# Normed rows of x by a product with a diagonal, later pad clearing, and projections of units 1 to 5 as three rounded products

## The reference, cut to what is computed

```python
h = rms_norm(x, norm1_w)
u = h @ w_in
rnn_x, rnn_gate, q, k, v, iq, ik, iw, g = jnp.split(u, offsets, axis=-1)
q = rms_norm(q.reshape(B, T, N_HEADS, HEAD_DIM), q_norm_w)     # 16 heads of 64
k = rms_norm(k.reshape(B, T, N_KV_HEADS, HEAD_DIM), k_norm_w)  # 4 heads of 64
ik = rms_norm(ik, idx_k_norm_w)
# index scores: relu(iq . ik) weighted by iw; the 64 best keys of each query are kept
# attention over them: softmax(q . k * scale) @ v
```

## Time and profile before

| | us |
|---|---|
| median of 3 runs (1203.43 to 1207.15) | 1205.72 |
| the profiled execution | 1205.84 |
| its span, first to last instruction | 1204.0 |
| TensorE busy | 1111.9 (92%) |
| VectorE busy | 501.4 (42%) |
| ScalarE busy | 396.3 (33%) |
| mean DMA rate over the span | 257 GB/s |

### The profile page before, as it was taken

How to read it: one execution, slowest core, us unless ns; L and a number is a source line. 1 busy time by engine, 2 the same in 40 slices (tenths; PEclk the granted TensorE clock), 3 DMA queues, 4 the chain that set the end, 5 groups by cost and what they waited for, 6 DMA issues and landing times.

```text
span 1204.0 us, 16125 instructions
## 1 busy us (share of the span) xinstructions
PE 1111.9 (92%) x6491; PEld 785.2 (65%) x6491; DVE 501.4 (42%) x965; ACT 396.3 (33%) x761; POOL 16.3 (1%) x28
## 2 busy tenths in 40 slices
PE   6999999999999999999999996998978897879786
PEld 5778898888999999798678885432323232323231
DVE  3657776586766655576975523000100010101011
ACT  2432665934666444565345402000100000001000
POOL 3000000000000000000000000000000000000000
PEclk9999999999999999999999998899999999999999
DMA  7444543244456676345223786699999999999996
GB/s 228 155 145 151 188 141 140 89 140 140 170 180 193 157 184 165 139 157 180 84 73 138 275 354 250 256 428 428 428 427 427 428 427 427 428 429 427 427 423 251
DMA packets 94066, 309.42 MB, mean 257 GB/s; under 512 B 6000, under 2 KB 39032, under 8 KB 82040
## 3 DMA queue, kind: packets, MB, share of 16 engines
q1 hardware_dynamic: 93256, 307.42, 66.2%
q0 software_dynamic: 496, 1.07, 0.4%
q10 hardware_dynamic: 256, 0.10, 0.0%
HBM read 307.53 MB, written 1.05 MB: 256 GB/s over the span
## 4 chain that ended last, share of the span: by engine, by line
PE 72%; DMA 22%; DVE 3%; ACT 1%; issue 1%; SPq 0%; ACTq 0%; DVEq 0%
PE bank L435 71%; DMA parts_room<-in_w_up 7%; DMA arena<-in_w_down 4%; DMA arena<-in_w_up 3%; DMA parts_room<-in_w_down 3%; DMA ring<-in_w_down 3%; DMA xh<-in_w_down 2%; PE bank L644 0%; DMA arena<-in_x 0%; DVE arena L1567 0%; DVE parts L1632 0%; DVE roots_room L1604 0%; PE bank L548 0%; DVE hidden_parts L1840 0%; DVE arena L2157 0%
## 5 line engine op out<-in xcount | busy, mean ns | idle before, releaser
L1228 ACT ACTIVATE parts<-ring 128x512 fp32r<-128x512 f32 x288 | 179.0, 629 | 196.5 <-PE bank L435 195.4
L1632 DVE TENSOR_TENSOR parts<-ring,parts 128x512 fp32r<-128x512 f32 x288 | 193.2, 690 | 117.2 <-ACT parts L1228 115.8
L435 PE MATMUL bank<-parts 128*128 128x256 f32 (+1 forms) x1872 | 239.8, 288 | 0.8 <-issue 0.6
L435 PEld LDWEIGHTS bank<-parts 128*128 128x128 f32 x1872 | 230.1, 191 | 13.2 <-issue 10.1
L435 PE MATMUL bank<-hidden_parts,parts 128*128 128x256 f32 x1024 | 164.9, 283 | 0.0
L435 PE MATMUL bank<-arena 128*32 128x512 f32 (+5 forms) x516 | 148.6, 499 | 9.2 <-DMA ring<-in_w_down 2.7
L435 PE MATMUL bank<-arena,roots_room 128*32 128x512 f32 x400 | 131.4, 601 | 12.1 <-DMA ring<-in_w_gate 3.7
L435 PEld LDWEIGHTS bank<-hidden_parts,parts 128*128 128x128 f32 x1024 | 141.4, 192 | 0.1
L2144 DVE TENSOR_TENSOR sqr<-bank,arena 128x512 f32<-128x512 f32 x8 | 5.2, 686 | 269.9 <-ACT arena L1531 269.9
L435 PEld LDWEIGHTS bank<-arena 128*128 128x128 f32 (+3 forms) x516 | 74.6, 192 | 54.6 <-issue 43.3
L435 PE MATMUL bank<-ring,roots_room 128*32 128x512 f32 x224 | 95.6, 593 | 7.8 <-DMA xh<-in_w_up 4.0
(11 more groups left out here) (298 smaller groups left out, 1068.0 us busy)
## 6 DMA issues: line engine op xcount, KB each, us to landing
ring<-in_w_in SPq DMA_DIRECT2D x22, 2048.0 KB, 8.0
arena<-in_w_gate SPq DMA_DIRECT2D x14, 2048.0 KB, 34.9
arena<-in_w_down SPq DMA_DIRECT2D x13, 2048.0 KB, 37.3
arena<-in_w_up SPq DMA_DIRECT2D x11, 2048.0 KB, 37.0
ring<-in_w_ff_in SPq DMA_DIRECT2D x8, 2048.0 KB, 7.9
ring<-in_w_ff_out SPq DMA_DIRECT2D x8, 2048.0 KB, 9.0
parts_room<-in_w_up SPq DMA_DIRECT2D x8, 2048.0 KB, 36.8
ring<-in_w_gate SPq DMA_DIRECT2D x7, 2048.0 KB, 34.6
```

The source lines that it names most:

```text
L435: return nc.tensor.matmul(o, lhsT=l, rhs=r, start=first, stop=last)
L1228: A(w_part[0][:, p % PIECES], piece_of(n, p), ACT.Copy).then_inc(S("pieces rounded"), 1)
L1632: X.tensor_tensor(w_part[1][:, p % PIECES], piece_of(n, p), w_part[0][:, p % PIECES].bitcast(F32), ALU.subtract).then_inc(S("pieces split" ...
```

## The change

1. Start: `xdiag` (two 128x128 diagonals with 1/rms of the tokens) takes the place of `xnormed`. The 16 transposes of normed rows become 16 float32 products `xtok` by `xdiag`. Two of the four groups of x transposes are made ahead of them, two behind. The first half of unit 0 is loaded by a DMA of its own, and half (0,0) waits for its four banks of `hT` one by one.
2. GpSimd clears `ikpad` and `kpad` only when the first vectors have been turned.
3. Units 1 to 5 become `dense_split`, so ACT and DVE round and split ten more halves, and `hT` is split at once.
4. Queries are no longer normed on DVE: ACT writes them to `qT` times the norm weight, `q1_stats` puts the mean squares of all heads with tokens on partitions (128x32), and 1/rms goes as `q1_scale` into the scale of the softmax.
5. `kpad` is filled by `pad_keys(g)`, two copies at a time, behind later halves; `select_keys` is cut into `select_rounds` and `key_bias` between the halves' rests. Index scores use bank 7 once only.

The core of the diff:

```diff
-            for b in range(4):
+            def turn_x(b):
                 ps = take(4 + b, ("x", b))
...
+            turn_x(0)
+            turn_x(1)
             for b in range(4):
                 ps = take(b, ("h", b))
...
-                        last = nc.tensor.transpose(ps[:, c:c + P], xnormed[:, t, k * P:k * P + P], ident)
+                        last = mm(ps[:, c:c + P], xtok[:, t, k * P:k * P + P], xdiag[:, t, :])
                 last.then_inc(S("h turned"), 1)
+            turn_x(2)
+            turn_x(3)
...
+            pe.wait_ge(S("first half loaded"), 16)
...
+                    if t == 0 and k % 2 == 0:
+                        wait_taken(("h", k // 2))
...
-            dense(1, 0, hT)
+            dense_split(1, 0, 0)
...
+            def q1_stats(i):
...
+                for j in range(2):
+                    for t in range(TT):
+                        c, at_c = j * T + t * P, 8 * i + 4 * t + 2 * j
+                        last = mm(ps[:, at_c:at_c + 2], sqr[:, i % 2, c:c + P], mean_64[:, 0:P:64])
...
-            dense(5, 1, hT)
+            dense_split(5, 1, 0)
...
-            A(xnormed[:, 0, :], xtok[:, 0, :], ACT.Copy, scale=xscale[:, 0:1]).then_inc(S("x 0 scaled"), 1)
+            A(xdiag[:, 0, :], ident, ACT.Copy, scale=xscale[:, 0:1]).then_inc(S("x 0 scaled"), 1)
...
             half(4, 0)
-            root_of(("heads", 5), 512, "head stats", 6)
+            act.wait_ge(S("head stats"), 6)
+            empty(A(q1_root, ps("q1 stats")[:, 0:32], ACT.Sqrt, bias=eps), "q1 stats")
+            round_half(8)
+            pad_keys(1)
             half(4, 1)
+            round_half(9)
+            pad_keys(2)
             half(5, 0)
-            round_half(0)
+            round_half(EARLY)
+            pad_keys(3)
             half(5, 1)
...
-            X.tensor_scalar(xnormed[:, 1, :], xtok[:, 1, :], xscale[:, 1:2], None, ALU.mult).then_inc(S("x 1 scaled"), 1)
+            X.tensor_scalar(xdiag[:, 1, :], ident, xscale[:, 1:2], None, ALU.mult).then_inc(S("x 1 scaled"), 1)
...
+            rest_of_half(6)
+            select_rounds(0, range(0, 8))
+            key_bias(0)
+            rest_of_half(7)
+            wait_taken("q1 stats")
+            link(X.reciprocal(q1_scale, q1_root))
+            link(X.tensor_scalar(q1_scale, q1_scale, SC1, None, ALU.mult))
+            select_rounds(1, range(0, 2))
+            rest_of_half(8)
+            select_rounds(1, range(2, 5))
+            rest_of_half(9)
+            select_rounds(1, range(5, 8))
+            key_bias(1)
+            rest_of_half(EARLY)
...
-            G.memset(kpad, 0.0)
-            G.memset(ikpad, 0.0)
-
-            pool.wait_ge(S("h turned"), 4)
+            pool.wait_ge(S("vectors 0 turned"), 1)
+            G.memset(ikpad, 0.0)
+            G.memset(kpad, 0.0)
```

More of the change, by code:

```diff
@@ L402, in done @@
             return S(dense_at[job][0]), dense_at[job][1]
-        split_halves = [(n, h) for n in range(6, 12) for h in range(2)]
+        split_halves = [(n, h) for n in range(1, 12) for h in range(2)]
+        EARLY = 10
         LATE = len(split_halves)
@@ L607, in index_scores @@
                 wait_taken((1, t // 2))
-                ps = take(4 + a % 4, ("index", a))
+                ps = take(4 + a if a < 4 else 4 + a % 3, ("index", a))
                 mm(ps[:, 0:2 * keys], iqT[:, t, q * P:q * P + P], ikpad[:, :, 0:keys]).then_inc(S("index scores"), 1)
-            dense(2, 0, hT)
+            dense_split(2, 0, 0)
             for a in range(4):
                 index_scores(a)
-            dense(2, 1, hT)
-            head_stats(2)
-            for a in range(4, 8):
+            dense_split(2, 1, 0)
+            for a in range(4, 7):
                 index_scores(a)
[L618 to L625, removed]
-            dense(5, 1, hT)
+            q1_stats(0)
+            dense_split(3, 0, 0)
+            index_scores(7)
+            q1_stats(1)
+            filter_layer(2)
+            dense_split(3, 1, 0)
+            q1_stats(2)
+            dense_split(4, 0, 0)
+            q1_stats(3)
+            dense_split(4, 1, 0)
+            dense_split(5, 0, 0)
+            dense_split(5, 1, 0)
             def att_scores(a):
@@ L1261, in _, with pad_keys @@
                 A(h_part[0][:, k, :], hT[:, k, :], ACT.Copy).then_inc(S("h rounded"), 1)
-            act.wait_ge(S("pads set"), 1)
-            wait_taken((0, 0))
-            for g in range(KV_HEADS):
+            round_half(0)
+            half(0, 0)
+            act.wait_ge(S("lambda ready"), 1)
+            A(lw[1], lw[1], ACT.Exp).then_inc(S("lambda exp"), 1)
+            hidden_sine(0)
+            half(0, 1)
+            act.wait_ge(S("ik"), 1)
+            A(sqr[0:64, 1, 0:T], ps("ik")[0:64, 0:T], ACT.Square).then_inc(S("head squares"), 1)
+            root_of(("heads", 0), 512, "head stats", 1)
+            round_half(1)
+            half(1, 0)
+            root_of(("heads", 1), T, "head stats", 2, 64)
+            round_half(2)
+            half(1, 1)
+            round_half(3)
+            hidden_sine(1)
+            def pad_keys(g):
                 for side in range(2):
@@ L1302, in _ @@
                 for j in range(4):
[L1303 removed]
+                    c = 8 * g + 4 * q + 2 * (j % 2) + j // 2
+                    A(prob[:, j, 0:keys], prob[:, j, 0:keys], ACT.Exp, bias=nmx[:, j:j + 1], scale=q1_scale[:, c:c + 1],
                       accum_out=rsum[:, j:j + 1]).then_inc(S("exps"), 1)
@@ L1576, in _, with rest_of_h @@
                 empty(X.tensor_copy(xT[:, 2 * b:2 * b + 2, :], pair(bank[4 + b][:, :])), ("x", b))
+            def rest_of_h(src, h_set, k):
+                dve.wait_ge(S("h rounded"), KD * h_set + k + 1)
+                X.tensor_tensor(h_part[1][:, k, :], src[:, k, :], h_part[0][:, k, :].bitcast(F32), ALU.subtract)\
+                    .then_inc(S("h split"), 1)
+            for k in range(KD):
+                wait_taken(("h", k // 2))
+                rest_of_h(hT, 0, k)
             dve.wait_ge(S("vectors 0 turned"), 1)
```

117 lines of the change are left out of this document (59 added, 58 removed).

## The result

The changed kernel takes **1194.31 us** (median of 4 runs, 1193.77 to 1196.45), the kernel before beside it 1205.74 us (1203.43 to 1207.15). The ratio is 0.9909, 95% interval 0.9895 to 0.9923: faster by 11.4 us. The forecast was 1196.0 us, range 1192.5 to 1200.5. The profiled execution took 1196.45 us, its span is 1194.5 us.

The account below looks back on a forecast made before the run. TensorE's queue was taken to bound the first 700 us, the experts' weights the part from 765 us on. 1205.84 - 1.6 - 10.2 + 0.45 + 1.55 = 1196.0 us, range 1192.5 to 1200.5.

Parts of the forecast that it names:

- Start: Up to half (0,0): eight x transposes, then products with small diagonals; half (0,0) near 15.2 instead of 16.79, gain 1.6 us.
- the step on DVE: At the start: DVE stands also while GpSimd issues DMAs, to 9.38; its diagonal comes at 9.6, TensorE waits 0.25 us.
- The rate at the start: In the 32 MATMULs with the diagonal: 19 pass at 0.213 us and 13 at 0.12; half (0,0) near 15.2.
- Ten halves: Units 1 to 5 on TensorE: ten halves shrink from 6.91 to 5.89 us each, gain 10.2 us.
- Statistics of queries: On TensorE, four times: 0.86 us each becomes 8 MATMULs of 0.95 us with the tail, nothing either way.
- DVE at (4,1): Key selection on DVE delays the first split piece of half (4,1); TensorE waits 0.45 us, ends 0 and 4.
- Key copies: Ahead of the first attention scores: TensorE waits 1.55 us for ACT's rounding of (6,0) and two last copies.
- Rival A: At the start: clock stays at the lower rate, 0.5 lost in place of 1.6 gained, 1198.1 us; chance 0.10.
- B: In the selection and index stretch: DVE becomes the bound, 4 us in place of 0.45, 1199.6 us; chance 0.13.
- C: At all ten halves: the four-piece room runs dry, TensorE waits 1.92 us each, slower at 1215.2 us; chance 0.05.
- D: At the experts: their stream does not start earlier, so the gain is given back, 1205.8 us; chance 0.04.
- The rule of the prediction: At the start, in SBUF access: VectorE's two-port modes and GpSimd exclude each other for a whole instruction; no separate size given.

Follow-up runs that it names:

- e2: Changed kernel with the old start (full-size scaled rows, plain transposes, all of x turned first), later pad clearing kept: 1191.78 us.
- e3: Changed kernel with the last two key copies, pad_keys(3), put ahead of ACT's rounding of half (6,0): 1193.53 us.
- e11: Changed kernel as it is, measured again: 1195.14 us.
- e5: Changed kernel with units 1 to 5 as float32 products again, without rounding and rests for them: 1202.27 us.
- e6: Changed kernel with two more 128x512 DVE products ahead of each of the rests of (4,1), (5,0), (5,1) and (6,0): 1198.03 us.
- e8: Changed kernel with pad_keys(3) ahead of rounding half (6,0), and two of eight selection rounds for query block 0 behind the rest of (4,1): 1192.45 us.
- e12: Changed kernel with full-size scaled rows and plain transposes in place of the diagonal, x still turned eight ahead and eight behind: 1197.06 us.
- e1: Kernel before with only the clearing of ikpad and kpad moved behind the first turned vectors: 1201.54 us (one run).
- e4: Changed kernel with GpSimd's two pad memsets back at their old early place: 1199.20 us (one run).

## Why the prediction held, and where it did not

Its sum had 9.8 us less; the trace has 10.86 at the product ahead of the experts, the medians 11.4.

- **Start: 1.6 predicted, 1.92 in the profile; right in size, wrong in its reason, and the size is in part luck.** Over six executions with this start half (0,0) begins at 14.87 to 16.20, mean 15.45, against 15.2 predicted. The step that failed is the one on DVE: it was said to stand also while GpSimd issues DMAs, and to deliver its diagonal at 9.6. It took 0.33 us at 8.40 in the midst of those issues, and the 0.25 us of wait behind two products never came. TensorE waited for ACT's diagonal instead, for which the sum had no wait: it was there at 8.86, not 8.5, and the products began at 9.01, 0.51 late, 0.31 of it because x landed later. Against this stood products that took 4.99 us and not 5.61. From the step on DVE followed the larger miss: the gain was booked to the diagonal, and that the later memsets alone free the full-size scaling (4.10 to 0.75 us) was not asked. By e2 it is worth 3.5 us more at half (0,0).
- **The rate at the start.** 19 slow MATMULs of 32 were assumed, 13 counted (to 29 in e3); upper-rate ones stood 0.112 apart, not 0.12. The range of ends (13.9 to 17.3) holds all six. Behind this stands what the Trainium skill says in TensorE: Matmul & The Clock Gate, section "Part 4: PE-mode transpose", that transposes don't count as activity. e2 speaks against it: there the rate rose at 9.5 us behind 15 transposes and nothing else. The Trainium skill, TensorE: Matmul & The Clock Gate, Part 1, section "What you observe", gives the moment of the rise a scatter of 0.5 us either way from run to run. The trace agrees that it scatters, but by more: six executions of this start have 11.9 to 15.0 us.
- **Ten halves: 10.2 predicted, 10.6 measured** (69.56 us before, 59.00 now, from row starts). The split halves took 5.90 us on average, as assumed (5.89). The error is on the float32 side: (1,0), (1,1) and (2,0) took 7.10, 7.10 and 7.01 us before, where every half was put at 6.91.
- **Statistics of queries: nothing, as said** (four of them cost 3.43 us before and 3.45 now, the waits left out). But the first split half comes 0.41 us sooner behind the 128x512 products ahead of it (33.72 to 34.17 in e11, 33.94 to 34.80 in e5), and another 0.19 sooner behind the first index scores (53.56 to 55.10, before 59.79 to 61.52). Together they are the 0.6 us that 10.86 has beyond 1.92 + 10.6 - 2.25.
- **DVE at (4,1): 0.45 predicted, 0.65 measured. Key copies: 1.55 predicted, 1.60 measured**, in the order foreseen; e3, e6 and e8 take each away or lengthen it alone.
- **Rival A** (lower rate throughout the start) is what happened in e12, another start. **B** is what e6 made, and there the cost was larger than the idle time, through the clock. DVE was busy 57.72 of 71.50 us in the changed kernel, less than the 63 of 70 predicted, so B had less ground than it was given. **C** and **D** fell: no wait at the other halves, and the experts start 10.86 us earlier.

The rule of the prediction from the Trainium skill, SBUF — State Buffer, section "SBUF: two separate sides", is that one of the two blocks the other. e1 and e4 agree: 0.75 us for the full size without memsets, 3.56 for an eighth of it with them. By the same section of the Trainium skill the engine that starts first holds the ports. That the rows don't show: DVE's row begins first, at 8.15 in e4, and the first memset's at 9.34, yet DVE's ends last.

## What to carry to other kernels

When an edit removes a wait, look what else in the same edit could have done so, and try each part alone: here the later memsets carried the gain, and the new start cost 3.5 us against the old one (e2). When an edit that takes something back changes two things, as e2 does, part them too. In this trace a float32 product has two MATMULs where a transpose has one, so a scaling that hides under other work should stay off TensorE. In a stretch where TensorE's queue is the time, put the small work that it waits for (copies, choices) ahead of the rounding for later halves, and judge edits by marks in the timeline, which repeat to 0.1 us where executions of one kernel differ by several.

## What had not been expected of the hardware

- One start, six executions, and the rate rose at 11.9 to 15.0 us, which moves half (0,0) by 1.3 us. What TensorE did before moves the rise (9.5 to 10.6 us behind plain transposes without a pause, 15.9 with 1.29 us of pause), while the granted clock reads 1.00.
- A wait of 2.11 us in the middle of steady work, behind eight MATMULs of two columns, was followed by some 3 us at a granted clock of 0.50, the 1.2 GHz level; waits of 0.65 (behind the same eight) and 1.60 us in the changed kernel were not.
- In e4 DVE's instruction began 1.19 us before the first memset's row and still ended with the last. Why it stood before that row, when in the changed kernel the same DMA issues did not hold it, stays open; GpSimd's rows are rough.
